# Hybrid encoder layer: first products prepared in another order, turned rows through DRAM on GpSimd's queue, four blocks of x kept in DRAM

## What is computed

```python
h = _rmsnorm(x, norm_w)                                  # x: 1 x 1024 x 2048
proj = einsum('bsd,df->bsf', h, w_in)
q_a, k_a, v_a, z_a, q_m, k_m, v_m, o_m, z_m, g = split(proj)
qa = _rope_partial(_rmsnorm(q_a, q_norm_w), cos, sin)    # 8 heads x 128, 32 dims turned
ka = _rope_partial(_rmsnorm(k_a, k_norm_w), cos, sin)
# three dilated bands of attention, mixed by their denominators, times silu(z_a)
# 4 heads of a two-way mLSTM with q_m, k_m, v_m and gates g, normed,
# times sigmoid(o_m) * silu(z_m)
y = concatenate([attn, hm])
return x + einsum('bsf,fd->bsd', y, w_out)
```

## Time and profile before

| | us |
|---|---|
| median of 3 runs (2059.7 to 2060.83) | 2060.79 |
| the profiled execution | 2060.51 |
| its span, first to last instruction | 2058.4 |
| PE busy | 1990.4 (97%) |
| DVE busy | 1300.3 (63%) |
| ACT busy | 848.7 (41%) |
| POOL busy | 174.0 (8%) |

### The profile page before, as it was taken

The page is one execution under the profiler, slowest core; times in us unless marked ns, Lnnn a source line. Parts: engine busy times, 40 slices in busy tenths (PEclk is TensorE's granted clock), DMA queues, the critical chain, the costliest instruction groups (busy, mean ns, idle before and its releaser), DMA issues.

```text
span 2058.4 us, 27134 instructions
## 1 busy us (share of the span) xinstructions
PE 1990.4 (97%) x9257; PEld 1626.8 (79%) x9257; DVE 1300.3 (63%) x2669; ACT 848.7 (41%) x1350; POOL 174.0 (8%) x156
## 2 busy tenths in 40 slices
PE   4999999999999999999998999999989999999999
PEld 3887788788888888888887878778777787778887
DVE  7777757768768768768778566575665544433222
ACT  5553325335335426335454253644536344242110
POOL 4340000110010010010000111010110000000000
PEclk9999999999999999999999999999999999999999
DMA  4552335564474465375354655364555625425443
GB/s 160 182 179 88 109 113 184 121 151 123 118 166 119 116 161 144 97 180 141 98 199 108 158 138 132 75 154 93 113 121 158 233 66 170 141 74 184 144 153 107
DMA packets 160551, 281.53 MB, mean 137 GB/s; under 512 B 18288, under 2 KB 39312, under 8 KB 160160
## 3 DMA queue, kind: packets, MB, share of 16 engines
q1 hardware_dynamic: 141984, 246.25, 37.3%
q0 software_dynamic: 18432, 33.56, 11.6%
HBM read 185.23 MB, written 92.41 MB: 135 GB/s over the span
## 4 chain that ended last, share of the span: by engine, by line
PE 87%; DVE 4%; issue 3%; ACT 2%; DMA 2%; SPq 1%; DVEq 0%; ACTq 0%
PE ps L714 18%; PE ps L718 18%; PE ps L716 18%; PE ps L742 5%; PE ps L743 5%; PE ps L744 5%; PE ps L925 3%; PE ps L894 2%; PE ps L863 1%; PE ps L819 1%; PE ps L828 1%; PE ps L911 1%; PE ps L822 1%; PE ps L929 1%; DVE w_lo L1190 1%
## 5 line engine op out<-in xcount | busy, mean ns | idle before, releaser
L714 PE MATMUL ps<-t_hi,w_hi 128*128 128x512 f32 x1792 | 717.5, 400 | 48.3 <-DVE t_lo L1644 12.4
L716 PE MATMUL ps<-t_lo,w_hi 128*128 128x512 f32 x1792 | 702.0, 392 | 0.0
L718 PE MATMUL ps<-t_hi,w_lo 128*128 128x512 f32 x1792 | 701.9, 392 | 0.0
L714 PEld LDWEIGHTS ps<-t_hi,w_hi 128*128 128x128 f32 x1792 | 338.8, 189 | 130.5 <-issue 64.1
L718 PEld LDWEIGHTS ps<-t_hi,w_lo 128*128 128x128 f32 x1792 | 338.7, 189 | 72.3
L716 PEld LDWEIGHTS ps<-t_lo,w_hi 128*128 128x128 f32 x1792 | 339.4, 189 | 65.8
L961 ACT CAST w_hi<-w_raw 128x512 fp32r<-128x512 f32 x256 | 158.4, 619 | 417.6 <-PE ps L718 200.8
L961 ACT CAST w_hi<-s_tmp 128x512 fp32r<-128x512 f32 x256 | 158.6, 620 | 268.2 <-PE ps L718 239.6
L1190 DVE TENSOR_TENSOR w_lo<-s_tmp,w_hi 128x512 fp32r<-128x512 f32 x256 | 182.3, 712 | 125.2 <-ACT w_hi L961 115.7
L1190 DVE TENSOR_TENSOR w_lo<-w_raw,w_hi 128x512 fp32r<-128x512 f32 x256 | 181.7, 710 | 119.9 <-ACT w_hi L961 113.5
L742 PE MATMUL ps<-t_hi,w_hi 128*128 128x512 f32 x384 | 155.7, 405 | 9.5 <-DVE xt L1635 9.5
(11 more groups left out here) (215 smaller groups left out, 2667.6 us busy)
## 6 DMA issues: line engine op xcount, KB each, us to landing
w_raw<-w_all_dram SPq DMA_DIRECT2D x320, 256.0 KB, 3.6
fin_dram<-xt SPq DMA_DIRECT2D x128, 256.0 KB, 4.2
fin_dram<-xt POOLq DMA_DIRECT2D x128, 256.0 KB, 4.5
arena<-fin_dram SPq DMA_DIRECT2D x64, 512.0 KB, 6.4
arena<-xT_dram SPq DMA_DIRECT2D x48, 256.0 KB, 5.8
arena<-xT_dram SPq DMA_DIRECT2D x16, 512.0 KB, 4.0
arena<-rs_dram SPq DMA_DIRECT2D x16, 512.0 KB, 5.9
y_raw<-y_dram SPq DMA_DIRECT2D x16, 512.0 KB, 5.1
```

The costliest lines, as they stand in the source:

```text
L714: nc.tensor.matmul(ps[:, bank, :], hi, t_hi[:, n, k, :], start=new and k == 0, stop=False, skip_group_check=True)
L716: nc.tensor.matmul(ps[:, bank, :], hi, t_lo[:, n, k, :], start=False, stop=False, skip_group_check=True)
L718: mm = nc.tensor.matmul(ps[:, bank, :], lo, t_hi[:, n, k, :], start=False, stop=k == KP - 1, skip_group_check=True)
```

## The change

- **The start.** SP loads the blocks `B12` and `B22` ahead of the weights of the second product. DVE makes the remainders of product 0, then `t_one` and `t_two`, and only then `s_one`, `s_two`, `weight_lo(1)`, `s_three`. ACT scales `B12`, `B11` and `B22` in a row ahead of `weight_hi(1)`; the scaling of `B11` was DVE's. One semaphore for a block in place of one for each tile of it, for `B12` and `B22`.
- **Blocks in DRAM.** `t_hi` and `t_lo` of products 1, 3, 4 and 5 (`KEPT`) are stored to `t_dram` at units 16 to 44, every fourth unit one transfer of 1 MB. In the third making they are loaded back; their scaling of `B12`, differences, casts and remainders are left out there (`build_sums` is for `b = 1` alone).
- **Turned rows.** The rotated pieces go from GpSimd's queue to `rot_dram` (at 4, 5) and, after landing, back to `raw_a`, `raw_b` (at 5, 6). The order of the dimensions of q, k, of the norm's weights and the tables is changed to fit (`TURNED`), so that two loads per tile do in place of four.
- **Attention's order.** v is loaded at 4 into a place of its own (`v_at`) and multiplied at 7; `normed` moves from 7, 9 to 8, 9; z's product from 8 to 10; the second broadcast from 5 to 6. The steps of softmax (`softmax_act`, `softmax_dve`) come first in a unit, ahead of emptying the bank and of the weights' parts.
- Some semaphores are merged (`a_mh` into `a_m`, `eps_out` into `rows_out`, the `x_` ones).

```diff
@@ -90
+KEPT = (1, 3, 4, 5)
@@ SP
                 sp.dma_start(stage[blk][:, kt, :], xT[at][:, half * HALF:(half + 1) * HALF]
-                             ).then_inc(b21_in if blk == B21 else b_in[blk][kt], 16)
+                             ).then_inc(b11_in[kt] if blk == B11 else b_in[blk], 16)
...
+            def t_stores(u):
+                i, rest = divmod(u - 16, 8)
+                if rest in (0, 4) and 0 <= i < len(KEPT):
+                    n = KEPT[i]
+                    sp.wait_ge(tl_done[n], t_made(n, 0))
+                    sp.dma_start(t_dram[i, rest // 4], flat_t((t_hi, t_lo)[rest // 4], n)).then_inc(t_out, 16)
+
+            def t_loads(u):
+                off = u - BUILD_AT[2]
+                if off - 2 in KEPT:
+                    n = off - 2
+                    i = KEPT.index(n)
+                    sp.wait_ge(prod, PRODUCTS * (STAGE[2] - 1) + n + 1)
+                    for part_, t in enumerate((t_hi, t_lo)):
+                        sp.dma_start(flat_t(t, n), t_dram[i, part_]).then_inc(t_in[i], 16)
...
                 for blk, at in ((B11, -13), (B12, -12), (B22, -11), (B21, -9)):
-                    if off == at:
+                    if off == at and (b, blk) != (2, B12):
...
                     for i, to in enumerate(turn):
                         src = fin[2 * GROUPS[g[i]][0] + 1 - i]
-                        for k in range(4):
-                            sp.dma_start(to[k * ROT:(k + 1) * ROT, 0:256],
-                                         src[k // 2, 0:ROT, k % 2 * 256:(k % 2 + 1) * 256]).then_inc(turn_in[i], 16)
+                        for k in range(2):
+                            sp.dma_start(to[k * 2 * ROT:(k + 1) * 2 * ROT, 0:256],
+                                         src[k, 0:ROT].rearrange("r (q n) -> (r q) n", q=2)).then_inc(turn_in[i], 16)
...
-                if at == 5:
+                if at in (5, 6):
+                    i = at - 5
                     sp.wait_ge(rs_out, 32 * (h + 1))
                     sp.wait_ge(a_ss, h + 1)
-                    for i, to in enumerate((a_q, a_k)):
-                        sp.dma_start(to, rs_dram[h, i].rearrange("r b n -> (r b n)").unsqueeze(0).to_broadcast([P, SEQ])
-                                     ).then_inc(bc_in, 16)
-                if at in (5, 6):
-                    i = at - 5
-                    raw, to = ((raw_a, turn[0]), (raw_b, turn[1]))[i]
-                    sp.wait_ge(a_rot, 8 * h + 4 * i + 4)
-                    for k in range(4):
-                        sp.dma_start(raw[0:ROT, k * 256:(k + 1) * 256], to[k * ROT:(k + 1) * ROT, 0:256]
-                                     ).then_inc(turned[i], 16)
+                    sp.dma_start((a_q, a_k)[i], rs_dram[h, i].rearrange("r b n -> (r b n)").unsqueeze(0)
+                                 .to_broadcast([P, SEQ])).then_inc(bc_in[i], 16)
+                if at == 4:
+                    if h > 0:
+                        sp.wait_ge(a_pv, 4 * h)
+                    tile_done(sp, g[0], 0)
+                    sp.dma_start(halves(v_at), fin_tile(g[0], 0)).then_inc(v_raw, 16)
...
-                if at == 8:
-                    sp.wait_ge(a_rope, 2 * h + 1)
-                    tile_done(sp, g[0], 0)
-                    sp.dma_start(halves(raw_a), fin_tile(g[0], 0)).then_inc(v_raw, 16)
...
             for kt in range(KP):
                 x_block(0, B11, kt)
+            for blk in (B12, B22):
+                for kt in range(KP):
+                    x_block(0, blk, kt)
             weights(0, 1, 0, 0)
             weights(0, 1, 1, 1)
-            for kt in range(KP):
-                x_block(0, B12, kt)
             weights(0, 0, 1, 4)
-            for kt in range(KP):
-                x_block(0, B22, kt)
@@ PE
-                if g in STAGE and not (g == 0 and n < 2):
+                if g == STAGE[2] and n in KEPT:
+                    pe.wait_ge(t_in[KEPT.index(n)], 32)
+                elif g in STAGE and not (g == 0 and n < 2):
                     pe.wait_ge(tl_done[n], t_made(n, STAGE.index(g)))
@@ ACT
+                    if (b, blk) == (0, B11):
+                        act.wait_ge(tl_done[0], kt + 1)
...
+                if b == 1 and n in KEPT:
+                    act.wait_ge(t_out, 32 * len(KEPT))
                 nc.scalar.copy(t_hi[:, n], t_src[n]).then_inc(th_done[n], 1)
...
-                    if off == at:
+                    if off == at and (b, blk) != (2, B12):
                         scale_x(b, blk)
-                if off in (1, 3, 4, 5, 6, 8, 9):
-                    t_high(b, {1: 0, 3: 2, 4: 1, 5: 3, 6: 4, 8: 6, 9: 5}[off])
+                n = {1: 0, 3: 2, 4: 1, 5: 3, 6: 4, 8: 6, 9: 5}.get(off)
+                if n is not None and not (b == 2 and n in KEPT):
+                    t_high(b, n)
...
+            def softmax_act(h, at):
                 if 0 <= at - 12 < 8:
                     normalised(h, at - 12)
...
+            for blk in (B12, B11, B22):
+                scale_x(0, blk)
             weight_hi(1)
-            scale_x(0, B12)
             for u in range(UNITS):
+                for h in range(ATT_HEADS):
+                    softmax_act(h, u - A_START[h])
                 if 1 <= u <= IN_UNITS:
                     evict(u - 1)
...
-                    scale_x(0, B22)
@@ DVE
+            def softmax_dve(h, at):
                 if 0 <= at - 12 < 8:
                     reciprocal(h, at - 12)
                 if 0 <= at - 11 < 8:
                     masked(h, at - 11)
+                if 0 <= at - 13 < 8:
+                    take_probs(h, at - 13)
...
-                if at == 8:
+                if at == 10:
                     dve.wait_ge(z_raw, 16 * (h + 1))
                     nc.vector.tensor_tensor(ystage, ystage, xrs[:], ALU.mult).then_inc(a_zs, 1)
-                if at == 10:
+                if at == 7:
                     dve.wait_ge(v_raw, 16 * (h + 1))
-                    nc.vector.tensor_tensor(raw_a, raw_a, xrs[:], ALU.mult).then_inc(a_vs, 1)
+                    nc.vector.tensor_tensor(v_at, v_at, xrs[:], ALU.mult).then_inc(a_vs, 1)
...
-                if at in (7, 9):
-                    normed(h, (at - 7) // 2)
+                if at in (8, 9):
+                    normed(h, at - 8)
...
-            s_one(0)
-            s_two(0)
-            s_three(0)
             for kt in range(KP):
                 dve.wait_ge(th_done[0], kt + 1)
...
-            weight_lo(1)
-            for kt in range(KP):
-                dve.wait_ge(tl_done[0], kt + 1)
-                nc.vector.tensor_scalar(stage[B11][:, kt, :], stage[B11][:, kt, :], ncol[:, kt:kt + 1], None, ALU.mult
-                                        ).then_inc(pre[B11], 1)
             for kt in range(KP):
                 t_one(0, kt)
+            for kt in range(KP):
+                t_two(0, kt)
+            s_one(0)
+            s_two(0)
+            weight_lo(1)
+            s_three(0)
             for u in range(UNITS):
+                for h in range(ATT_HEADS):
+                    softmax_dve(h, u - A_START[h])
...
                 if u == 0:
-                    for kt in range(KP):
-                        t_two(0, kt)
@@ POOL
+            def turned_rows(h, at):
+                if at in (4, 5):
+                    i = at - 4
+                    pool.wait_ge(a_rot, 8 * h + 4 * i + 4)
+                    pool.dma_start(rot_dram[h, i], turn[i][:, 0:256]).then_inc(rot_out[i], 16)
+                if at in (5, 6):
+                    i = at - 5
+                    pool.wait_ge(rot_out[i], 16 * (h + 1))
+                    pool.wait_ge(a_sq, 2 * h + 2)
+                    pool.dma_start(halves((raw_a, raw_b)[i][0:ROT]),
+                                   rot_dram[h, i].rearrange("(s r q) n -> r s (q n)", s=2, q=2)).then_inc(turned[i], 16)
...
                     added(g, n) if g < NG or n < 2 else None
+                for h in range(ATT_HEADS):
+                    turned_rows(h, u - A_START[h])
@@ data
+TURNED = [i + s * (ROT // 2) for i in range(ROT // 2) for s in range(2)]
```

More of the change, by code:

```diff
@@ L635, in _ @@
                         mlstm_loads(j, u - M_START[j])
+                    t_stores(u)
+                    t_loads(u)
                     for b in (1, 2):
@@ L1531, in rotate @@
                 nc.vector.memset(spare[:, 0:1], 0.0)
-                nc.vector.stream_shuffle(to[:, 256:512], to[:, 0:256], mask=[(r + ROT // 2) % ROT for r in range(ROT)]
+                nc.vector.stream_shuffle(to[:, 256:512], to[:, 0:256], mask=[r ^ 2 for r in range(ROT)]
                                          ).then_inc(a_rot, 1)
@@ L1811 @@
     for h in range(ATT_HEADS):
-        cols += [a[:, P * h:P * (h + 1)] for a in (va, qa, ka, za)]
+        turned = [P * h + i for i in TURNED + list(range(ROT, P))]
+        cols += [va[:, P * h:P * (h + 1)], qa[:, turned], ka[:, turned], za[:, P * h:P * (h + 1)]]
     wo = w_out[0].reshape(2, D_MODEL // 2, D_MODEL)[::-1].reshape(D_MODEL, D_MODEL)
@@ L1819 @@
```

(6 more changed lines are left out.)

140 lines of the change are left out of this document (72 added, 68 removed).

## The result

| | before | after |
|---|---|---|
| median us | 2060.24 (4 runs, 2057.34 to 2060.83) | 2044.68 (4 runs, 2043.3 to 2046.71) |
| the profiled execution | 2060.51 | 2045.27 |
| its span | 2058.4 | 2043.5 |

The ratio is 0.9932, 95% interval 0.9916 to 0.9947: faster by 0.5 to 0.8%. Forecast were 2032 us and 28.7 us of gain; 15.6 came by the medians, 14.9 by the two spans. The time lies inside the range, but about half of the gain is missing.

What follows compares the result with a forecast made beforehand. TensorE was taken as the bound, busy 1990.4 of 2058.4 us, so only idle time and lower-clock products could change. Attention -24.3, third building -4.8 and start +0.4 made -28.7 from 2060.51: 2032 us, range 2024 to 2046.

Steps and rivals of the forecast that it cites:

- its upper end, 29.1 us: Attention: the largest gain reckoned, with ACT's wait going too; the forecast itself was -24.3 us.
- At the median, store and load of tile 0 end at 1516.1 + 8.6: Attention, fifth head: tile 0's turned rows are back from DRAM at 1524.7 us, at a median 4.3 us a trip.
- 3 us off for heads later than the median: Attention: 3 us taken off 27.3 for heads whose chain lands later than the median, leaving -24.3 us.
- rival 1: Attention: turned rows come no sooner through DRAM, so half the gain stays, -12, 2044 us; chance 15%.
- the minima had a price of their own, 2.3: Attention: PE's 2.3 us of waits for row minima go, since masks and reciprocals stand ahead of emptying banks.
- The last difference ends at 19.1: Start: after ACT's twelve scalings, 10.8 to 18.5 us, differences end at 19.1; second product near 23.9, 1.3 us later.
- GpSimd's four differences: Start: the upper end, +4 us, if DVE waits up to 1.27 us for each of these differences.
- a term for the clock in attention: Attention: 6.5 us come back from products that ran at the lower clock after waits, 2.4 and 4.1.
- That makes 27 us of 29: Third building: eight 1 MB loads take 27 us of 29 before the last block is wanted; -4.8 us holds, narrowly.
- rival 2: Start or third building: the port costs time or the last load is late, +4 or +5, 2036 us; chance 13%.
- Rival 3: Attention: softmax ahead of emptying delays the bank, 0.7 us in each of 64 units, 45 us, 2077 us; chance 2%.
- Rival 4: Attention: waits at z and turned rows are replaced by equal ones at the broadcasts, -4, 2057 us; chance 3%.

Runs made afterwards that it cites:

- a_sbuf_copies: The changed kernel with turned rows copied inside SBUF on SP's queue, four copies a tile, no way through DRAM: 2032.5 us.
- a_start_old: The changed kernel with the start in the old order on all engines and SP, the rest as changed: 2041.6 us.
- b_start_old_copies: The changed kernel with both the old start order and the turned rows copied inside SBUF on SP's queue: 2029.6 us.
- a_diff_held: The changed kernel with one wait more: GpSimd's first four differences wait for DVE's remainders of the second product: 2043.6 us.
- b_softmax_only: The kernel before the change with only the order of softmax changed, its steps first in a unit: 2055.5 us.
- c_normed_old: a_sbuf_copies with the normalisations back at units 7 and 9 of a head instead of 8 and 9: 2042.5 us.
- b_pool_copies: The changed kernel with turned rows copied inside SBUF, four copies a tile, issued on GpSimd's queue: 2032.1 us.
- c_v_late: a_sbuf_copies with v loaded at unit 8 and multiplied at 10 as before, into its own place: 2038.8 us.

## Why the prediction missed

**Attention, right in what went, wrong in how soon rows come.** The waits that it named are the ones that fell, from 22.6 to 8.0 us; its upper end, 29.1 us, is near what attention gives once the rows come by copies (29.2), partly by luck: it had 22.6 us of waits and 6.5 of clock, and the waits fell by 20.2 there, so 9.0 came behind them. The step that failed is "At the median, store and load of tile 0 end at 1516.1 + 8.6". The 4.3 us of a trip came from accumulating stores that are spread over the whole input, while here the DMA engines are 0.94 to 1.03 busy: a store took 4.9 and a load 5.4 at the median, 6.0 and 6.1 in the last head. The rows that would have told it stood there: the broadcasts of the same units took 5.9, at most 9.6 us. The forecast took 3 us off for heads later than the median, but the last four, not single ones, were at 11.0 to 13.3 us for two trips. It took rival 1's mechanism for 15% and got it in the last heads.

**What the text did not price.** Four things of the change in attention could be tested one by one, and the forecast costed the waits that they were to remove together, not each part (only the minima had a price of their own, 2.3). The runs part them. By what attention loses when each is taken from a_sbuf_copies, three are gains: the later place of the normalisation 10.0 us, v's early load 5.3, softmax first 4.3. The fourth, the way through DRAM, is a loss: 10 to 14 us against copies, by the four kernels that have it. Two pairs differ in nothing else, and their medians say 12.2 (the change and a_sbuf_copies) and 11.9 (a_start_old and b_start_old_copies). The three gains make 19.6 of 29.2 us. The other 9.6 no run parts: z's product at unit 10 instead of 8, the second broadcast a unit later, two small loads for four, each tile's copies right behind its own broadcast, or what two parts do only together.

**The start, +7.2 for +0.4.** The step that failed is "The last difference ends at 19.1"; it ended at 22.4. Its own upper end named the place ("GpSimd's four differences"), with a price of +4. I held it unlikely, because in the kernel before GpSimd had been the one that waited, 8.88 us for one difference while DVE ran on at 0.68. In the new order three `t_two` and a weight sum took 1.07 us more each, 4.3 us, and a_diff_held took them away again; by unit 4, 2.8 of them were left in the lag (4.1 against 1.4). The other 3 us are the clock, which the sum for the start did not have at all, although it had a term for the clock in attention. With neither, in a_diff_held, the start cost 1.4.

The Trainium skill, SBUF — State Buffer, section "SBUF: two separate sides", has it that a DVE instruction with two SBUF inputs contends with a GpSimd instruction that reads SBUF, and that the one that starts first has the port pair for its whole instruction while the other fully blocks. The trace agrees that both engines suffer: 0.68 became 1.75 on DVE and 1.27 became 1.71 on GpSimd. Why GpSimd got no turn in the kernel before, and every second one here, no run settles. That ACT's scalings paced DVE here isn't enough: the last of them ended at 18.48, and DVE's operations from 18.96, 20.64 and 22.30, which waited for nobody by their rows, still took turns.

**The third building, 3.2 for 4.8.** The waits went as named. The step that was too small is "That makes 27 us of 29": the eight loads took 30.6. PE waited 0.2 to 2.5 us for the last one in all ten traces that keep blocks, and in one of them that with the clock behind it took the gain back almost whole (-0.5). In the other nine it gave 3.2 to 4.4 us.

**The rivals.** Two came true in part and together, and neither had been given with the other. Attention (18.9, and 15.1 to 15.9 in the other three traces of it) lies between the forecast (24.3) and rival 1 (12), and rival 2's place cost 7 where it said 4 or 5. That the time is nearly rival 1's 2044 is chance: rival 1 kept the forecast's +0.4 for the start, where 7.2 came, and 12 for attention, where 18.9 came, and the two errors, 6.8 and 6.9 us, cancel. Rival 3, softmax ahead of the bank, is refuted: alone it gains. Rival 4 is out.

## What to carry to other kernels

Take the price of a transfer from a row of the stretch where it will run, and look at the DMA share there first: with the DMA engines full, each of two dependent trips took 5.5 to 7.5 us in the last three heads, and a copy in one trip beat the way in two by 12 us. When work on DVE is moved earlier, ask what GpSimd does at that moment; holding back what nobody waited for made the start 5.8 us shorter in the trace, though the medians show only 1.0. Cost a package part by part even where the parts serve one end: here one of four was a loss of 12 us that the others hid.

## What was unexpected

- DVE and GpSimd, both on 128x512 additions from SBUF, took turns evenly: 1.75 and 1.71 us each, against 0.69 and 1.27.
- At the start, the clock fell to 0.57 to 0.60 after a wait of 2.6 us in some kernels and stayed at 1.00 after the same 2.6 us in the kernel before, in b_softmax_only and in c_normed_old. A fall costs some 3 us with the second one that follows it, and 1.6 us where no second one followed (b_pool_copies, c_v_late). Kernels whose first units are the same came out both ways (+4.6 and +7.2), so it is not settled what decides it.
- Eight loads of 1 MB issued within 17 us landed 4.7 to 5.0 us after their issue at first and 12.6 to 15.0 us at last, over ten traces.
